# Second mixer: who makes the low parts, where the forget-sum levels and the attention heads stand in the rounds

## The reference, cut to what matters

```
u = rms_norm(x) @ w_in                      # hq hf hi hg | aq ak av | sz sxbc sdt
# 1. HGRN2, 4 heads of 64: forget = lb + (1-lb)*sigmoid(f); log_f = log(forget); key = 1-forget
b = cumsum(log_f)                           # the "forget sums"
a[t,s] = sum_k q[t,k] * key[s,k] * exp(b[t,k]-b[s,k])   for s <= t
o = a @ hi ; rms_norm per head ; * silu(g)
# 2. attention, 6 heads of 64: q, k normed per head, bias from a table, softmax, @ v
# 3. Mamba2, 6 heads of 64: xbc = silu(causal conv of 4 taps(xbc) + bias); decay products; norm
x = x + concat(1, 2, 3) @ w_out
```

## Time and profile before

| | us |
|---|---|
| median of 3 runs (lowest to highest) | 2533.14 (2532.22 to 2534.16) |
| the profiled execution's own time | 2529.74 |
| its span, first to last instruction | 2527.8 |
| TensorE busy | 2422.8 (96%) |
| VectorE busy | 1846.2 (73%) |
| ScalarE busy | 1255.1 (50%) |
| GpSimd busy | 380.4 (15%) |
| mean granted TensorE clock | 0.984 |

### The profile page before, as it was taken

One profiled execution on the slowest core, in us unless ns is written; L12 is line 12 of the kernel. 1 busy time (PEld: TensorE's weight loads), 2 busy tenths in 40 slices (PEclk: granted clock), 3 DMA queues, 4 the chain that ended last, 5 costly groups with the idle time before them and its releaser, 6 DMA issues.

```text
span 2527.8 us, 39274 instructions
## 1 busy us (share of the span) xinstructions
PE 2422.8 (96%) x15670; PEld 2108.4 (83%) x15670; DVE 1846.2 (73%) x3600; ACT 1255.1 (50%) x1793; POOL 380.4 (15%) x310
## 2 busy tenths in 40 slices
PE   7998798999899999999999999899999999999999
PEld 7987778988878888888888888888878888788887
DVE  8787946656645798888887555744798888888555
ACT  3544545445445555555444545454555545444444
POOL 3023321003423700000000001441720000000000
PEclk9999999999999999999999999999999999999999
DMA  9696524654324445444445555224445444444554
GB/s 388 203 368 220 192 103 170 217 200 159 117 98 171 161 173 184 167 168 166 174 177 206 188 195 192 107 94 161 176 153 196 168 167 169 165 171 180 204 196 150
DMA packets 73030, 455.77 MB, mean 180 GB/s; under 512 B 9099, under 2 KB 15371, under 8 KB 20754
## 3 DMA queue, kind: packets, MB, share of 16 engines
q1 hardware_dynamic: 72162, 452.21, 49.7%
q0 software_dynamic: 688, 1.06, 0.3%
HBM read 449.17 MB, written 4.06 MB: 179 GB/s over the span
## 4 chain that ended last, share of the span: by engine, by line
PE 78%; DVE 15%; ACT 3%; issue 2%; POOL 1%; DMA 1%; SPq 0%; DVEq 0%; POOLq 0%; ACTq 0%
PE ps L349 16%; PE ps L351 16%; PE ps L350 16%; PE ps L376 15%; PE ps L378 6%; DVE wlo L331 4%; PE ps L2523 2%; ACT whi L312 1%; DVE AC L2703 1%; PE ps L395 1%; DVE raw L342 1%; PE ps L375 1%; DVE T L2699 1%; DVE AST L2837 1%; DVE XB L1200 1%
## 5 line engine op out<-in xcount | busy, mean ns | idle before, releaser
L312 ACT ACTIVATE whi<-raw 128x1024 fp32r<-128x1024 f32 x765 | 809.2, 1060 | 1052.9 <-PE ps L351 648.1
L331 DVE TENSOR_TENSOR wlo<-raw,whi 128x1024 fp32r<-128x1024 f32 x657 | 806.5, 1233 | 480.8 <-ACT whi L312 480.5
L376 PE MATMUL ps<-HT,whi 128*128 128x512 f32 x2048 | 723.7, 401 | 13.5 <-POOL wlo L331 7.3
L378 PE MATMUL ps<-HT,wlo 128*128 128x256 f32 x1792 | 503.2, 281 | 0.0
L376 PEld LDWEIGHTS ps<-HT,whi 128*128 128x128 f32 x2048 | 374.7, 189 | 85.6 <-issue 11.6
L349 PE MATMUL ps<-whi,CH 128*128 128x512 f32 x1024 | 404.6, 395 | 4.8 <-DVE AST L2837 4.8
L350 PE MATMUL ps<-wlo,CH 128*128 128x512 f32 x1024 | 399.2, 390 | 0.0
L351 PE MATMUL ps<-whi,CL 128*128 128x512 f32 x1024 | 399.1, 390 | 0.0
L378 PEld LDWEIGHTS ps<-HT,wlo 128*128 128x128 f32 x1792 | 339.8, 190 | 7.9
L331 POOL TENSOR_TENSOR wlo<-raw,whi 128x1024 fp32r<-128x1024 f32 x108 | 264.6, 2452 | 329.5 <-ACT whi L312 329.5
L349 PE MATMUL ps<-HT,whi 128*128 128x256 f32 x968 | 280.6, 290 | 8.1 <-DVE wlo L331 4.2
(11 more groups left out here) (394 smaller groups left out, 3357.7 us busy)
## 6 DMA issues: line engine op xcount, KB each, us to landing
raw<-in_down SPq DMA_DIRECT2D x128, 1024.0 KB, 4.8
raw<-in_up SPq DMA_DIRECT2D x128, 1024.0 KB, 4.8
raw<-in_w_in SPq DMA_DIRECT2D x41, 1024.0 KB, 4.9
raw<-in_ffn_gu SPq DMA_DIRECT2D x36, 1024.0 KB, 4.9
raw<-in_w_ada SPq DMA_DIRECT2D x28, 1024.0 KB, 6.6
raw<-in_ffn_d SPq DMA_DIRECT2D x22, 1024.0 KB, 5.5
raw<-in_w_out SPq DMA_DIRECT2D x12, 1024.0 KB, 4.8
raw<-in_w_ada SPq DMA_DIRECT2D x16, 512.0 KB, 12.5
```

Source lines behind the costliest of these rows:

```text
L312: e.activation(self.whi[:, i % NSPLIT, :], self.raw_of(i), ACT.Copy, bias=0.0, scale=1.0).then_inc(*k.inc("w_hi", ("hi", i)))
L331: e.tensor_tensor(self.wlo[:, n, :], self.raw_of(i), self.whi[:, n, :].bitcast(F32), ALU.subtract).then_inc(*k.inc("w_lo_pool" if pool els ...
L376: t = e.matmul(out.rearrange("p (a t) -> p a t", a=2), hi[:, s], self.HT[:, :, c, :], start=c == 0, stop=c == 7)
L378: t = e.matmul(out[:, 0:T], lo[:, s], self.HH[:, c, :], start=False, stop=False)
```

## The change

What it does:
- VectorE makes the low parts of all slots of both second mixers; GpSimd makes none there.
- The first tap of the convolution, with the bias, is made by ScalarE straight from the projected block; VectorE makes the other three.
- `decays` of levels 1 to 8 stand in rounds 3, 5, 6, 8, 9, 11, 13 and 15 (before: 3 to 10), and `products` of a level in the round after its decays (before: two rounds after). Level 0 stays in round 4.
- The piece v0 is projected before i (the host lays the weights out in that order).
- The heads start in round 23 and there are 33 rounds.

```diff
 ON_POOL = set(range(1, 14, 2)) | set(range(71, 100, 2))
-for _s in (165, 465):
-    ON_POOL |= set(range(_s + 2, _s + 31, 2))
 for _s in (201, 501):
...
-    def conv_dve(self, e, what, need, out, src, w, b):
+    def conv_dve(self, e, what, need, out, src, w, b=None):
         k = self.k
-        for x in k.late(*need):
-            e.wait_ge(*x)
-        e.tensor_scalar(out, src, w(3), b, ALU.mult, ALU.add).then_inc(*k.inc("dve_conv", (*what, 3)))
+        if b is not None:
+            for x in k.late(*need):
+                e.wait_ge(*x)
+            e.tensor_scalar(out, src, w(3), b, ALU.mult, ALU.add).then_inc(*k.inc("dve_conv", (*what, 3)))
         for j in (2, 1, 0):
             n = 3 - j
-            for x in k.late((*what, j + 1)):
+            for x in k.late((*what, j + 1), *need):
...
-        t.n_heads, t.first_head, t.hides = 6, 26, False
+        t.n_heads, t.first_head, t.hides = 6, 23, False
...
-        t.toks = ("z1", "z", "g", "qk0", "qk1", "qk2", "i", "v0")
-        t.rounds = 36
+        t.toks = ("z1", "z", "g", "qk0", "qk1", "qk2", "v0", "i")
+
+        t.levels = {3: 1, 5: 2, 6: 3, 8: 4, 9: 5, 11: 6, 13: 7, 15: 8}
+        t.rounds = 33
...
@@ mixer2_pe @@
-            if 4 <= r < 13:
-                products(r - 4)
+            if r == 4:
+                products(0)
+            if r - 1 in t.levels:
+                products(t.levels[r - 1])
...
@@ mixer2_act @@
                 if name == "xr":
+                    for w in k.late(("used", i), ("c2", l)):
+                        e.wait_ge(*w)
+                    e.activation(t.XB[:, c, :], PS[:, b, 0:T], ACT.Identity, bias=self.vec2(l, "conv_b")[:, c:c + 1],
+                                 scale=self.vec2(l, "conv_w")[:, 21 + c:22 + c]).then_inc(*k.inc("act_proj", (tag, "xc", c, 3)))
                     evict((tag, "xr", c), [("used", i)], t.XR[:, c, :], PS[:, b, 0:T])
...
-            if r == 12:
+            if t.levels.get(r - 1) == 8:
                 for par in range(2):
...
-            if 3 <= r < 11:
-                decays(r - 2)
+            if r in t.levels:
+                decays(t.levels[r])
...
@@ mixer2_dve @@
                 self.conv_dve(e, (tag, "xc", c), [(tag, "xr", c)], t.XB[:, c, :], t.XR[:, c, :],
-                              lambda j: w[:, 7 * j + c:7 * j + c + 1], cb[:, c:c + 1])
+                              lambda j: w[:, 7 * j + c:7 * j + c + 1])
...
-            if 4 <= r < 12:
-                products(r - 4)
-            if 3 <= r < 11:
-                decays(r - 2)
+            if r == 4:
+                products(0)
+            if t.levels.get(r - 1, 8) < 8:
+                products(t.levels[r - 1])
+            if r in t.levels:
+                decays(t.levels[r])
...
@@ lay (host) @@
-        pieces += [slice(hi, hi + 256), slice(av, av + 256)]
+        pieces += [slice(av, av + 256), slice(hi, hi + 256)]
```

More of the change, by code:

```diff
@@ L2198, in proj @@
             if r in t.chans and t.chans[r][0] == "xr":
-                c, w, cb = t.chans[r][1], self.vec2(l, "conv_w"), self.vec2(l, "conv_b")
+                c, w = t.chans[r][1], self.vec2(l, "conv_w")
                 self.conv_dve(e, (tag, "xc", c), [(tag, "xr", c)], t.XB[:, c, :], t.XR[:, c, :],
-                              lambda j: w[:, 7 * j + c:7 * j + c + 1], cb[:, c:c + 1])
+                              lambda j: w[:, 7 * j + c:7 * j + c + 1])
         def decays(lev):
```

## The result

The kernel with the change takes **2542.52 us** (median of 5 runs, 2542.12 to 2546.61), the kernel before on the same chip 2532.22 (5 runs, 2530.48 to 2534.16): ratio **1.0046, interval 1.0033 to 1.0058**. It is slower by about 10 us; the forecast was 2531.1. The profiled execution took 2542.12 with a span of 2540.3, so 12.5 more than the span before.

The account below looks back on a forecast made before the run. TensorE, busy 96%, was taken as the bound, with time to gain only where it stands or is throttled. +0.9 - 1.1 - 2 x 1.4 + 1.0 = -2.0 us from 2533.14 gave 2531.1 us, range 2521 to 2541.

Parts of the forecast that it names:

- stretch at full clock: Rounds 5 to 16, each mixer: 51.9 us of TensorE work plus 11.0 of waits, 62.9 us.
- Clock ... +1.0: Both second mixers: one slow stretch at 1.2 GHz in one mixer, +1.0 us; ends 0 and +10.
- rival 2: Waits of 2.36 us behind levels 2 and 4 bring the clock down in both mixers: +7.0, 2540.1 us; chance 0.12.
- a PEclk below 0.95 in the first part: Sign of being wrong: TensorE's granted clock under 0.95 in rounds 5 to 16, meaning slow clock in both mixers.
- What a slow block costs: Time at 1.2 GHz in the mixers: half its length is lost, 1.8 us in the first, 5 in the other.
- Level 3: Round 6: VectorE starts late from the level before, so TensorE waits 0.7 us for the level's products.
- The tail: Heads after round 26: earlier heads move 3.35 us out and shorten the standing; -1.4 us per mixer.
- The order v0, i: Projection of v0 before i: both there as early as needed, transfers alike, so 0.
- The low parts: Both second mixers: 17 us of low parts come to VectorE, GpSimd's blocks go, rounds 4 to 10 need 29.7 against 30.2.
- Here the gain is spent: Levels: products one round after sums meet a 5.4 us VectorE chain; waits of 11.0 us against 8.2 before.
- The first tap: Convolution's first tap on ScalarE: nothing waits for it, taken as 0; from above 2.5 us per mixer.
- rival 3: Table loads in rounds 13, 15, 16 hold ScalarE twice 1.28 us: 7.7 above the forecast, 2538.8 us; chance 0.03.

Follow-up runs that it names:

- e1: Changed kernel with unused matmuls filling TensorE's waits for levels 1, 2, 4, 6, 7 and 8: 2532.56 us, 1.0000 against the kernel before.
- e11: e1 with ScalarE's exponential of the softplus issued in round 7 instead of round 5: 2526.59 us, one run.
- e5: Changed kernel with unused matmuls in front of the waits for levels 2 and 4 only, 10 each: 2544.96 us, 1.0041 against the kernel before.
- e10: Changed kernel with unused matmuls in front of the waits of levels 1, 3, 6, 7 and 8, none at 2 and 4: 2539.70 us, 1.0033.
- e8: Kernel before with unused matmuls in front of TensorE's waits for levels 3, 4, 5 and 7, nothing else changed: 2526.05 us, 0.9979.
- e13: e3 with the heads begun in round 26 and 36 rounds, v before i kept: 2512.21 us, 0.9921 against the kernel before.
- e4: Changed kernel with every second low part on GpSimd again: 2549.42 us, 1.007 against the kernel before.
- e9: e3 with every second low part on GpSimd again: 2519.19 us, 0.9946 against the kernel before.
- e2: Changed kernel with a level's products two rounds after its sums, levels still spread: 2513.06 us, 0.9932 against the kernel before.
- e3: Changed kernel with products two rounds after the sums and levels 1 to 8 back in rounds 3 to 10: 2509.26 us, 0.9914.
- e7: e3 with the convolution's first tap on VectorE again, not on ScalarE: 2516.48 us, 0.9937 against the kernel before.

## Why the prediction was wrong

Its stretch by stretch sum against the profile, per mixer:

| step | forecast | measured |
|---|---|---|
| waits at levels 1, 2, 4 | 0.35, 2.36, 2.36 | 0.32, 2.51, 2.57 |
| levels 6, 7, 8, then XS | 0.9, 1.6, 0.7, 1.65 | 1.07, 1.73, 0.64, 1.23 |
| level 3, level 5 | 0.7, 0.35 | 1.99 with the slow blocks gone (e1), none |
| stretch at full clock | 62.9 | 62.8 (e11) + 1.3 for level 3 |
| rounds 17 to 26, tail | 43.6, 17.5 | 43.9, 18.2 |
| clock, both mixers | +1.0 | 8.1 + 4.2 = 12.3 (after against e11) |
| starts of the two mixers | -0.65, -1.2 | -1.7, none |

The forecast was -2.0, and the profiled executions differ by +12.4. Of these 14.4 us the clock makes 11.3, level 3 2.6 and the tails 1.0; the small rest lies at the starts, at the ends and in rounding.

- **The step that failed is "Clock ... +1.0".** It measured +12.3, beyond its own upper end of +10 (like the forecast, this counts from 62.9 us at full clock in both mixers; less the 1.3 that the clock had cost before, the change in it is 11.0). Its own sign of being wrong, a PEclk below 0.95 in the first part, came at 0.83. It compared single waits: 2.36 lay nearer to 3.7 than to none, so one slow block. The runs show repeated standing in its place: 10 us of waits in seven or eight places brought 23.9 and 13.7 us at 1.2 GHz, e5 and e10 with a part of the places left brought 10 to 20 per mixer, and e11, with nearly all filled, none. This is rival 2 (0.12, 2540.1 us): its condition was some 10 us at 1.2 GHz in both mixers, and its sign and time were nearly right. The argument against it, that the first mixer's three other waits had brought no second fall, was one case and weighed too much. The other mixer of the kernel before spoke against it: its clock fell twice, the second time right behind a wait of 1.85 us (PE's timeline and the stretches of before):

```profile
1621.89 1.60 PE L1884 MATMUL ps<-QK 64*128 64x64 f32 x16 [1.85 <-DVE QK L2225]
```

```profile
1610.50:1621.90 11.40, 9.55 (x84) 8.94 (x82) 10.98 (x23) 4.61 (x9) 3.02 (x3) 1.00 0.27 93
1621.90:1628.00 6.10, 6.10 (x42) 5.90 (x42) 5.47 (x14) 0.66 (x1) 0.00 (x0) 0.72 0.06 8
```

- **What a slow block costs** was wrong too. The prediction took half its length, 5 us for the other mixer; the profiled executions of before and e8 show 1.3, as the next wait gave the rest back. After the change about a third was lost: 8.1 us for 23.9 and 4.2 for 13.7. Why more than before is not shown.
- **Level 3** (0.7) left out that ScalarE's queue waits for VectorE: the softplus' exponential stands in front of the high parts. e11 moved it and the wait became 0.67. In the kernel after the wait itself was 0 and 0.49, since slow blocks took its place.
- **The tail** was -1.4 per mixer and is -0.9. MIX's transposes no longer wait for VectorE, but for i's eviction by ScalarE, which moved behind v0's (waits of PE in the tail, 728 to 746.3 us, against the earlier trace rows):

```profile
PE ps L1149 <- DVE ML L2370: 0.9, 1, 0.9
PE ps L1982 <- ACT HV L2017: 0.8, 1, 0.8
PE ps L1141 <- DVE DG L1185: 0.2, 1, 0.2
```

  The order v0, i had been priced at nothing; by e13 it costs about 0.3, if the low parts play no part in the tail. The three waits on PT went, where the prediction still had h1's values waiting for PT; with the heads three rounds later they are there (e13). What TensorE stands in the tail, 18.20 - 16.16 = 2.0 us, is near the forecast 17.7 - 15.45 = 2.25; its own work was set 0.7 too low.
- **The low parts** were right in kind: the taps that took 3.71 us beside GpSimd all take 1.51 now (VectorE's timeline):

```profile
621.47 1.23 DVE L329 TENSOR_TENSOR wlo<-raw,whi 128x1024 fp32r<-128x1024 f32 x1 [2.54 <-ACT whi L310]
622.61 1.51 DVE L1199 SCALAR_TENSOR_TENSOR XB<-XR,c,XB 128x255 f32<-128x255 f32 x3
```

  The Trainium skill (SBUF — State Buffer, Who interferes with whom) says that a VectorE instruction with two SBUF inputs and a GpSimd instruction that reads SBUF share a port under an exclusive lock, the second standing until the first ends; the 3.71 before and the 1.51 now agree. What it costs here is the 7 to 10 us of e4 and e9.
- **"Here the gain is spent"** held: with the products two rounds behind (e2, e3) the gain appears, 20 to 24 us under before. That it also keeps the clock up was not foreseen.
- **The first tap** at 0 was the price of the tap on ScalarE, and no run shows that price by itself; what leaves VectorE, 0.44 us a round, had gone into the chain. e7 shows the two together in e3: 7.2 us gained, near the 14 x 0.44 = 6.2 that leave VectorE. In the kernel after it was not tried alone.
- **Table loads** (rival 3) fell. Four more per mixer came, nine for five, as forecast, and cost no more than their length. ScalarE's timeline of after:

```profile
678.19 1.28 ACT L2067 ACT_TABLE_LOAD   x1
679.49 0.42 ACT L2067 ACTIVATE EB<-SF 128x256 f32<-128x256 f32 x1
```

  The activation starts 1.30 after the load, as in the earlier trace rows; the wait at level 8, behind such a load, is 0.64 of 0.7. The drain of the Trainium skill (ScalarE: Activation LUTs, What ACT_TABLE_LOAD costs) does not show here either.

**Open:** which pattern of waits takes the clock down. Beside the table under e10, one of 1.9 us did so in both mixers (e7), one of 0.96 in e2 with 3.4 us at 1.2 GHz, one of 0.54 in e3 did not. And e5 with 7.7 us of waits had more at 1.2 GHz in the second mixer (20.5) than the kernel after with 10 (13.7), and the two mixers of after differ by 10 us at the lower level with like waits. Nothing here tells this apart.

## What to carry to other kernels

An in-order consumer one round behind a chain longer than a round turns each step into a wait; count the chain (here 5.4 us) against the distance (3.07, or 6.1 with two rounds) before spreading work. On TensorE do not price the clock by the longest wait: here neither the longest nor the sum of the waits gave it. Test the clock's part apart from the rest by filling the waits with matmuls that nothing uses; if that gains, shorten the chain. And a queue's small instruction that waits for another engine is a wait for everything behind it.

## What was not expected of the hardware

- Matmuls that do nothing made the kernel 10 us faster (after 2542.5, e1 2532.6) and the kernel before 5 us faster (e8, 0.9979).
- TensorE fell to 1.2 GHz behind waits of 0.96 (e2) to 2.6 us with work on both sides, and in after, from 615.9 us, where it had stood for 0.32 only (granted clock 0.54 from 615.7 to 619.4). There a matmul of 128x256 shows 0.41 us instead of 0.28, and a block takes 5.16 us instead of 3.1.
- A ScalarE activation from PSUM with a scale and a bias per partition takes 0.547 us (L2039, 14 times), the plain copy of the same 128x256 0.37 (L2017) and one with a scale alone 0.48.
